# Hybrid backbone step on one core: loads and copies of the DeltaNet heads in another order, and the left half of the output projection begun inside the last head

## The reference, cut to what matters

```python
def deltanet_mixer(h, w_in, conv_w, a_log, dt_bias, norm_g, w_out, s0):
    proj = h @ w_in                                   # q, k, v, z of 8 heads, and gates
    qkv, z, ab = jnp.split(proj, [QKV_W, QKV_W + HV], axis=-1)
    qkv = jax.nn.silu(short_conv(qkv, conv_w))
    q, k, v = jnp.split(qkv, [HK, 2 * HK], axis=-1)
    ...
    o_f, s_f = chunk_gated_delta(q, k, v, g[:, :, 0], beta[:, :, 0], s0[:, 0])
    o_b, s_b = chunk_gated_delta(flip(q), flip(k), flip(v), flip(g[:, :, 1]), flip(beta[:, :, 1]), s0[:, 1])
    o = o_f + flip(o_b)
    o = o * lax.rsqrt(jnp.mean(o * o, axis=-1, keepdims=True) + EPS) * norm_g
    o = o * jax.nn.silu(z.reshape(B, L, N_HEADS, HEAD_V))
    y = o.astype(h.dtype).reshape(B, L, HV) @ w_out   # the output projection
    return y, jnp.stack([s_f, s_b], axis=1)

def run_trunk(x, cond, dn_state0, rows, p):           # layer 0 shown
    mod = jax.nn.silu(cond) @ p['ada_w'][i] + p['ada_b'][i]
    sh1, sc1, g1, sh2, sc2, g2 = jnp.split(mod[:, None, :], 6, axis=-1)
    y, s = deltanet_mixer(x * (1.0 + sc1) + sh1, ...)
    x = layer_norm(ALPHA * x + g1 * y, p['ln_g'][i, 0], p['ln_b'][i, 0])
    y = swiglu(x * (1.0 + sc2) + sh2, p['ffn_w_gu'][j], p['ffn_w_down'][j])
    x = layer_norm(ALPHA * x + g2 * y, p['ln_g'][i, 1], p['ln_b'][i, 1])
```

## Time and profile before

| | us |
|---|---|
| three runs | 2220.36, 2223.6, 2232.7 |
| median | 2223.6 |
| the profiled execution, whole | 2243.42 |
| its span (first to last instruction) | 2241.6 |
| PE busy | 1988.6 (89%) |
| DVE / ACT / POOL busy | 980.4 / 764.8 / 804.6 |
| mean granted clock of TensorE (1 is 2.4 GHz) | 0.955 |

### The profile page before, as it was taken

How to read it: one execution, slowest core, us unless ns; L and a number is a source line. 1 busy time by engine, 2 the same in 40 slices (tenths; PEclk the granted TensorE clock), 3 DMA queues, 4 the chain that set the end, 5 groups by cost and what they waited for, 6 DMA issues and landing times. The chain is left out here.

```text
span 2241.6 us, 39883 instructions
## 1 busy us (share of the span) xinstructions
PE 1988.6 (89%) x14992; PEld 1598.5 (71%) x14993; DVE 980.4 (44%) x1616; ACT 764.8 (34%) x1243; POOL 804.6 (36%) x486
## 2 busy tenths in 40 slices
PE   5889899899898699999999998889998898899990
PEld 2778778778787546888788876668786686677770
DVE  3345555555566345432322238443233333332228
ACT  2323323333333102222122202364445545544331
POOL 0054243342353203212111133564346546543234
PEclk7999999999999899999999999999999999999995
DMA  8132232332331424324322441785658758765354
GB/s 275 29 107 86 84 107 67 103 108 63 107 100 47 174 104 140 98 81 144 104 94 85 133 142 51 249 291 188 191 178 260 245 177 273 226 198 161 114 174 155
DMA packets 264225, 320.08 MB, mean 143 GB/s; under 512 B 25801, under 2 KB 206289, under 8 KB 263979
## 3 DMA queue, kind: packets, MB, share of 16 engines
q1 hardware_dynamic: 249115, 284.95, 39.9%
q10 hardware_dynamic: 10832, 16.96, 2.1%
q0 software_dynamic: 4032, 14.68, 1.7%
HBM read 283.87 MB, written 32.65 MB: 141 GB/s over the span
## 5 line engine op out<-in xcount | busy, mean ns | idle before, releaser
L1349 POOL TENSOR_TENSOR wlo<-wring,whi 128x1024 fp32r<-128x1024 f32 x182 | 460.2, 2531 | 768.5 <-ACT whi L1824 704.2
L1140 PE MATMUL pp<-whi,xTh 128*128 128x512 f32 (+1 forms) x1152 | 448.3, 389 | 40.1 <-POOL wlo L1349 13.1
L1824 ACT ACTIVATE whi<-wring 128x1024 fp32r<-128x1024 f32 (+1 forms) x324 | 316.0, 982 | 452.0 <-PE pp L1142 364.1
L1142 PE MATMUL pp<-wlo,xTh 128*128 128x512 f32 (+1 forms) x1152 | 432.9, 376 | 0.0
L1141 PE MATMUL pp<-whi,xTl 128*128 128x512 f32 (+1 forms) x1152 | 432.3, 375 | 0.0
L2431 DVE TENSOR_TENSOR wlo<-wring,whi 128x1024 fp32r<-128x1024 f32 (+1 forms) x180 | 222.5, 1236 | 214.3 <-ACT whi L1824 126.5
L1140 PEld LDWEIGHTS pp<-whi,xTh 128*128 128x128 f32 x1152 | 219.4, 190 | 96.3 <-issue 32.1
L1142 PEld LDWEIGHTS pp<-wlo,xTh 128*128 128x128 f32 x1152 | 219.0, 190 | 39.9
L1141 PEld LDWEIGHTS pp<-whi,xTl 128*128 128x128 f32 x1152 | 219.9, 191 | 34.5
L1140 PE MATMUL pp<-whi,hTh 128*128 128x512 f32 x528 | 212.7, 403 | 9.2 <-POOL wlo L1349 3.1
L1142 PE MATMUL pp<-wlo,hTh 128*128 128x512 f32 x528 | 206.6, 391 | 0.0
(11 more groups left out here) (327 smaller groups left out, 2964.6 us busy)
## 6 DMA issues: line engine op xcount, KB each, us to landing
wring<-in_moe_w_gu SPq DMA_DIRECT2D x320, 256.0 KB, 3.8
wring<-in_ada_w SPq DMA_DIRECT2D x80, 512.0 KB, 4.9
wring<-in_moe_w_down SPq DMA_DIRECT2D x160, 256.0 KB, 3.5
wring<-in_ffn_w_gu SPq DMA_DIRECT2D x80, 256.0 KB, 3.1
wring<-in_dn_w_in SPq DMA_DIRECT2D x128, 128.0 KB, 2.9
wring<-in_ffn_w_down SPq DMA_DIRECT2D x40, 256.0 KB, 3.1
expert_in<-zeros SPq DMA_DIRECT2D x36, 256.0 KB, 3.3
wring<-in_ada_w SPq DMA_DIRECT2D x32, 256.0 KB, 5.5
```

Source lines behind the costliest of these rows:

```text
L1140: pe.matmul(out, hi[:, c0 + c, tt], wh, start=(first and c == 0), stop=False)
L1142: mm = pe.matmul(out, hi[:, c0 + c, tt], wl, start=False, stop=(last and c == nk - 1))
L1349: pool.tensor_tensor(wlo[:, hs, 0:nk, 0:w], wring[:, ring_p.slot(k), 2:2 + nk, 0:w], whi[:, hs, 0:nk, 0:w].bitcast(F32), ALU.subtract).the ...
L1824: act.activation(whi[:, hs, 0:nk, 0:w], wring[:, ring_v.slot(k), 2 * s:2 * s + nk, 0:w], ACT.Copy)\
```

## The change

Four parts.

1. **SP**: the fills behind steps b = 0, 1, 2, 3 are now behind b = 0, 1, 3, 4; b = 2 has none. Where the list of chunks ends (in heads 6 and 7), three loads of `w_out` take the places.
2. **ACT**: `chunk_high` of the first chunk of head h + 2 moves from `scan(h)` into `inversion(h)`, behind the last `vt_copy` and ahead of `z_silu`; that of the second moves to the end of `scan(h)`, ahead of `out_square`.
3. **POOL and DVE**: `chunk_low` of the second chunk of each head moves from POOL to DVE, behind `update(h, 3)` of the inversion in which it is used.
4. **Output projection**: `w_out` is loaded by half slots (row pairs of two heads, 512 KB). A unit `out_unit(n, t, h)` is one matmul 128x512. For the left half, heads 0 to 5, tiles 0 to 3: 12 units stand where the projection of a next head would, in `inversion(7)`, and 12 between the steps of `scan(7)`. Tile 4 follows the scan, ahead of `out_columns(7)`; head 6 behind it, head 7 once `oT` is complete. The right half is unchanged in order, with banks of its own, so that only tile 3 waits for DVE (for all of the left residuals). The right weights of heads 4 to 7 are loaded once the units of tile 4 are done.

```diff
+def out_bank(n, t):
+    return (5, 7, 4, 6, 0)[t] if n == 0 else (1, 2, 3, 0, 4)[t]
...
@@ SP @@
             for hd in range(H):
-                for b in range(BURSTS):
+                for b, ahead in enumerate((2, 3, None, 4, 5)):
                     i = 2 * (BURSTS * hd + b) + RING
                     ada_loads(i, min(i + 2, 2 * BURSTS * H))
-                    q = CHUNKS * (hd + 1) + b + 2
-                    if b < CHUNKS and q < CHUNKS * H:
+                    q = CHUNKS * (hd + 1) + (ahead or 0)
+                    if ahead and q < CHUNKS * H:
                         chunk_fill(q)
+                    elif ahead and q < CHUNKS * H + RING:
+                        k = q - CHUNKS * H
+                        sp.wait_ge(S["slot_free"], 2 * (KD + CHUNKS * H + k + 1))
+                        out_load(k, 0, 0, 2 * k)
+            sp.wait_ge(S["ada_ps"], 1 + BURSTS * H)
+            out_load(0, 1, 0, 6)
+            out_load(1, 1, 1, 0)
+            out_load(2, 1, 1, 2)
...
@@ PE, inversion @@
                 def proj(lo, hi):
                     if nx:
                         project(h + 1, lo, hi)
+                    else:
+                        out_early(12 * lo // 32, 12 * hi // 32)
@@ PE, scan @@
                 adds(h, 0)
+                early(0, 2)
...
                 reads(h, 1)
+                early(2, 3)
...
@@ PE, after the heads @@
+            for h in range(6):
+                mm = out_unit(0, T - 1, h)
+            mm.then_inc(S["slot_free"], 4)
             out_columns(H - 1)
+            out_loaded(0, 1)
+            pe.wait_ge(S["oT_ready"], H)
+            for t in range(T):
+                out_unit(0, t, 6)
...
             pe.wait_ge(S["oT_ready"], H + 1)
-            for a in range(2):
-                gemm5(a, 4, lhs_o, 4 * a, a == 0, a == 1, S["res_ps"])
+            for t in range(T):
+                out_unit(0, t, H - 1).then_inc(S["res_ps"], 1)
...
             for t in range(T):
-                pe.wait_ge(S["res_step"], 2 * (t + 1))
+                if t == 3:
+                    pe.wait_ge(S["res_step"], 2 * T)
@@ POOL @@
                 if h + 2 < H:
                     chunk_low(CHUNKS * (h + 2))
-                    chunk_low(CHUNKS * (h + 2) + 1)
@@ ACT, inversion @@
                 vt_copy(h, 13)
+                if h + 2 < H:
+                    chunk_high(CHUNKS * (h + 2))
                 if nx:
                     z_silu(h + 1)
@@ ACT, scan @@
-                if h + 2 < H:
-                    chunk_high(CHUNKS * (h + 2))
-                    chunk_high(CHUNKS * (h + 2) + 1)
...
                     q_squares(h + 1)
+                if h + 2 < H:
+                    chunk_high(CHUNKS * (h + 2) + 1)
                 out_square(h)
@@ DVE, inversion @@
                 update(h, 3)
+                if nx:
+                    chunk_low(CHUNKS * (h + 1) + 1)
```

More of the change, by code:

```diff
@@ L540, in _ @@
             sp.dma_start(x[:, 1:T, :], A["x_sample"][0].rearrange("(t p) d -> p t d", p=P)).then_inc(S["x_in"], 16)
[L541 to L545, removed]
+            for half in range(2):
+                out_skip(3, half)
+            sp.wait_ge(S["slot_free"], 2 * RING + 2 * (KD + CHUNKS * H) + 4)
+            for k in (4, 5):
+                out_load(k, 0, 1, 2 * k - 4)
+                out_skip(k, 1)
+            ring.base += CHUNKS * H + OUT_SLOTS
             def zero_rows(e, k):
@@ L677, in slot @@
                 return ring.slot(k)
[L679 to L691, removed]
             pe.wait_ge(S["consts_in"], 16)
@@ L923, in out_columns, with out_loaded, out_unit, out_early @@
                 mm.then_inc(S["ogT_ps"], 1)
+            out_ring = Ring()
+            out_ring.base = KD + CHUNKS * H
+            def out_loaded(k, half):
+                pe.wait_ge(slot_loaded[out_ring.slot(k)][half], out_ring.loaded(k))
+            def out_unit(n, t, h):
+                k, row = out_weight(n, h)
+                return pe.matmul(bank(out_bank(n, t)), oT[:, h, t * P:(t + 1) * P], wring[:, out_ring.slot(k), row, :],
+                                 start=(h == 0), stop=(h == H - 1))
+            def out_early(lo, hi):
+                for i in range(lo, hi):
+                    t, h = i // 6, i % 6
+                    if i == 0:
+                        pe.wait_ge(S["ex_ready"], 4 * H)
+                        pe.wait_ge(S["v_ready"], H)
+                        pe.wait_ge(S["oT_ready"], 6 + 1)
+                    if i < 6 and h % 2 == 0:
+                        out_loaded(h // 2, 0)
+                    out_unit(0, t, h)
             def inversion(h):
@@ L999, in scan, with early @@
                 nx = h + 1 < H
+                def early(lo, hi):
+                    if not nx:
+                        out_early(12 + lo, 12 + hi)
                 pe.wait_ge(S["r_ready"], h * 4 + 4)
@@ L1016, in scan @@
                 adds(h, 1)
+                early(3, 5)
                 if nx:
@@ L1019, in scan @@
                 reads(h, 2)
+                early(5, 6)
                 if nx:
@@ L1022, in scan @@
                 adds(h, 2)
+                early(6, 8)
                 if nx:
@@ L1025, in scan @@
                 reads(h, 3)
+                early(8, 9)
                 if nx:
@@ L1028, in scan @@
                 adds(h, 3)
+                early(9, 11)
                 if nx:
@@ L1031, in scan @@
                 reads(h, 4)
+                early(11, 12)
                 if nx:
@@ L1078, in _ @@
             pe.wait_ge(S["oT_ready"], H + 1)
-            for a in range(2):
-                gemm5(a, 4, lhs_o, 4 * a, a == 0, a == 1, S["res_ps"])
+            for t in range(T):
+                out_unit(0, t, H - 1).then_inc(S["res_ps"], 1)
             pe.wait_ge(S["res_ps"], T)
-            pe.sem_inc(S["slot_free"], 2)
-            s2, s3 = slot(2), slot(3)
+            pe.sem_inc(S["slot_free"], 4)
             for t in range(T):
-                pe.wait_ge(S["res_step"], 2 * (t + 1))
-                for k in range(KD):
-                    mm = pe.matmul(bank(t), lhs_o(k, t), wring[:, s3 if k > 3 else s2, k % 4, :], start=(k == 0), stop=(k == KD - 1))
+                if t == 3:
+                    pe.wait_ge(S["res_step"], 2 * T)
+                for h in range(H):
+                    if t == 0 and h % 2 == 0:
+                        k, row = out_weight(1, h)
+                        out_loaded(k if h < 4 else k + RING, row // 2)
+                    mm = out_unit(1, t, h)
                 mm.then_inc(S["res_ps"], 1)
@@ L1425, in _ @@
             chunk_low(0)
-            chunk_low(1)
             pool.wait_ge(S["gate_step"], 12)
@@ L1430, in _ @@
             chunk_low(CHUNKS)
-            chunk_low(CHUNKS + 1)
             for h in range(H):
```

41 lines of the change are left out of this document (28 added, 13 removed).

## The result

The changed kernel takes 2173.77 us (median of 4 runs, 2172.05 to 2176.81) against 2228.15 for the kernel before on the same chip: ratio 0.9759, 95% interval 0.9721 to 0.9797, 54.4 us less. The forecast was 56.5 less and 2167, the range 2151 to 2189.

What follows compares the result with a forecast made beforehand. Heads 0 to 5 were held bound by burst and copy waits with slow matmuls behind, the end by DVE and its row loads. Heads -43, last head +4.5, end -18: -56.5 from 2223.6, forecast 2167 us, range 2151 to 2189.

Steps and rivals of the forecast that it cites:

- The burst wait: Heads 0 to 5: PE waits 20.7 us ahead of fifth bursts, their ada loads queued behind SP's third fill; would go.
- contention with the later fill: Fifth burst's load in each head: margin 1.6 us less some contention with a fill 3 us later; taken as zero.
- the rival of a busy memory: Heads 0 to 5: the 20.7 us are the load itself and stay; total -26.5, 2197 us; chance 0.08.
- The copy wait: Scans of heads 0 to 5: 13.9 us, as two `chunk_high` on ACT precede the copy `gram_k` needs; would go.
- The standstill of DVE: Heads: DVE blocked beside POOL, 0.8 us per head at three convolution products, 0.3 at the moved `chunk_low`.
- the strict reading: DVE and POOL port lock: moved subtractions and neighbours could cost DVE some 2 us more per head, 12 in sum.
- The last head: Head 7 with 24 units inside: inversion +2.7, scan +5.7, 4 taken back by the clock; 4.5 us more, bounds 0 and 11.
- The 4 us of clock: Head 7, inversion and scan: fewer PE pauses would win back 4 of some 6 us lost to slow matmuls.
- Behind the last head: From the scan's end to tile 4's residual: start falls from S + 79.9 to about S + 62, 18 us less.
- the bound set to none: Row loads behind the last head: 1 MB of right weights beside them could delay them up to 4 us; none taken.
- Part 4 as a whole: Output projection: last head 4.5 us more, 18 us less behind it; the end gives 13.5.
- The 20 us: Whole kernel: the profiled execution (2243.4) lay 20 us above the runs' median, 2223.6; the sum was set against the median.

Runs made afterwards that it cites:

- the SP order alone: Only SP's order of the fills changed, against the kernel before: 2192.91 against 2224.71, ratio 0.9862.
- second profile of before: The kernel before, unchanged, profiled once more: that execution took 2220.1 us, the median beside it 2224.71.
- heads alone: SP's fill order and the chunk copies and subtractions changed, old output projection kept, against the kernel before: 2179.49 us, ratio 0.9797.
- the projection alone: The kernel before with only the new output projection, fills and chunk copies as before: 2227.54 against 2228.71, ratio 0.9985.
- the kernel with the later products: The changed kernel with DVE's six row products moved behind the five left residuals: 2162.31 us, ratio to before 0.9718.
- the fastest kernel: The changed kernel with DVE's row products behind the left residuals and POOL's `chunk_low` ahead of `k_scale`: 2158.24 against 2222.03, ratio 0.9705.

## Why the prediction was right, point by point

- **The burst wait** went entirely, by the queue's order, as the SP order alone shows (32 us of the 45). No contention with the later fill was found: each fifth burst starts without a wait. Right, and the rival of a busy memory is out.
- **The copy wait** fell from 13.9 to 2.6 us over six heads (0.3 in each of heads 1 to 5, 0.9 in head 0). Neither moved `chunk_high` costs anything: ACT's stays of 1.06 us end at 553.55 and 585.59, and PE's waits name neither.
- **The standstill of DVE** was taken as 0.8 and 0.3 us per head; it is 0.54 at the three products (3.27 against 2.73) and nothing for PE at the other place. There `chunk_low` on DVE takes 1.22 us, but `out_gated` behind it takes 1.89 us where it takes 0.83 alone, and POOL's pair of products 4.08 where the next pair takes 2.49; nobody on PE waits for either. So DVE loses 1.6 us per head in all (1.1 taken, and 2 by the strict reading), but only 0.54 of it lies on PE's path. Heads: 43 forecast; 43.8 to 47.4 in the profiles, by which execution of before is taken, and 45 by the medians of the kernel without part 4.
- **The last head** was to cost 4.5. It costs 3.0 against the first profile of before and 7.0 against the second. The second is the one to go by, since all four other profiles with the old projection show 37.8 to 38.4 us of inversion and none the 42.4 of the first. So this term was too small by 2.5. Inversion: +3.7 (2.7 forecast). Scan: its step grew from 2.96 to 4.36 us as worked out, four times 1.4, but it is only 3.4 longer, since its first 40 matmuls, now at full clock, take 4.70 us instead of 6.84. The 4 us of clock came as busy time of PE, but only some 2 of them shorten the path; the prediction took off all 4. In the second profile of before (windows of the inversion and the scan) PE is busy for 25.39 + 16.90 us:

```profile
708.26:746.10 37.84, 25.39 (x726) 19.32 (x726) 21.12 (x41) 4.99 (x13) 20.66 (x19) 0.88 0.32 103
746.10:766.92 20.82, 16.90 (x112) 15.40 (x112) 8.27 (x32) 3.37 (x6) 0.00 (x0) 0.89 0.85 310
```

  After it is 35.50 + 23.28: 16.5 more for 24 units that are 20.6 at full clock, so 4.1 came back. The scan's first 40 matmuls in the two (timelines):

```profile
746.10 6.84 PE L752 MATMUL pp<-scratch 128*128 128x128 f32 x40 [0.66 <-DVE scratch L2171]
```

```profile
705.17 4.70 PE L775 MATMUL pp<-scratch 128*128 128x128 f32 x40 [0.66 <-DVE scratch L2249]
```

- **Behind the last head** 18 was too much: 15.0. The mechanism held, with PE's pause of 12.03 us (10.5 forecast) released by DVE. The step that failed is the bound set to none: the rows come 2.8 us later (23.1 us behind the scan's end, 20.3 before), because not only the right weights but everything behind them in SP's queue moves up. And 1.0 us more go to the slow matmuls after the pause (8.01 against 7.03), plus 0.9 for the first transposes (1.97 against 1.04 to 1.09); the sum had no slow matmuls there. From the rows to the end of `h_row(0)` DVE took 24.2 us instead of the 25.4 worked out, which took some of it back.
- **Part 4 as a whole** was priced at 13.5 as if it could be had by itself. By itself it gives 1 to 3 us; in the changed kernel it gives some 8, since heads alone are at 0.9797 and all four parts at 0.9759. The two intervals just touch, but head 7 and the stage behind it agree: 138.5 us in the profile with the old projection, 130.5 in the changed kernel. The prediction saw that the fills of head 7 were replaced by loads of `w_out`, but did not follow them through the old order of SP, where they would have blocked head 6's fifth burst.
- **The 20 us** by which the profiled execution of before lay above the median were for the most part in the rest: 1387.1 us behind residual(1, 4) against 1371.2 in the next profile, with 3.5 more in heads 0 to 5 and 4.0 in head 7. To set the sum against the median was right.
- **The total** came within 2 us of the forecast partly by luck. By the medians of the heads and the stages it is -45 + 7 - 15 = -53, against -43 + 4.5 - 18: the heads gave 2 more, the last head cost 2.5 more, the end gave 3 less. The bounds were also added up wrong: those named (0 to 3 us per head, 0 to 1, last head 0 to 11) reach from 2156 to 2191, not from 2152 to 2186, and leave out the 1 us per head that the text sets for the second `chunk_high` (2197 with it). The measured time lies inside either.
- **Open:** the rest. It takes 1377 to 1379 us in the changed kernel and the variants with its projection, 1372 and 1374 in the two fastest of them and 1383.5 in the projection alone; with the old projection it takes 1370 to 1374, but for the 1387.1 of the first profile. The first SwiGLU has 1 to 3 us of it where it was read. The ring of weights is entered at another slot there; whether that is the cause wasn't tried. For the same reason the stages don't add up to the medians exactly: against the second profile of before they give -43.8 + 7.0 - 15.3 = -52.1, the rest +6.7 and the start -0.8, in all -46.2, the difference of the two spans; that execution was 4.6 us under the median of its kernel. The 54.4 is a figure of medians, and the split among stages is known to some 5 us.

## What to carry to other kernels

A wait that the profile puts down to "issue" ahead of a matmul that reads loaded data can be a load queued behind another that waits for something else: set the issue time in the DMA queue beside the start of the reader, and when a queue's order is changed or new transfers are put in, follow each wait that now stands ahead of an urgent load, in every iteration, those at the end too. Before PE work is moved forward, look which engine bounds the place that it leaves: here DVE waited for all eight row loads to do work that needed only the first two, and moving one block of DVE gave 12 us, the whole early half of the projection some 8. Fillers put early between the steps of a recurrence lengthen it (3 to 4 us for 12 units here), and give nothing back while PE has a pause later on that could hold them: here the kernel's median was 7 us lower without them.

## What the runs showed of the hardware that was not expected

**A fall of the clock without a longer pause ahead of it.** Some heads take 79.83 instead of 78.30 us with the same waits. In the kernel with the later products, the 4 us on both sides of the border between heads 3 and 4, and of that between heads 4 and 5 (windows, columns as above):

```profile
427.68:431.68 4.00, 3.47 (x32) 3.27 (x30) 2.94 (x9) 3.08 (x5) 1.28 (x2) 1.00 0.00 0
431.68:435.68 4.00, 4.00 (x21) 3.16 (x21) 3.60 (x7) 0.31 (x1) 1.69 (x1) 0.66 0.52 142
...
507.51:511.51 4.00, 3.47 (x31) 3.27 (x30) 2.94 (x9) 3.09 (x5) 1.27 (x2) 1.00 0.00 0
511.51:515.51 4.00, 4.00 (x29) 3.16 (x29) 3.59 (x7) 0.31 (x1) 1.69 (x1) 1.00 0.57 147
```

PE was busy for 3.47 us of the four ahead of the border in both places. In the one the granted clock then is 0.66 (part of the stretch at 1.2 GHz), in the other it stays at 1.00. It costs 1.53 us. Heads 1 to 6 of both profiles of the changed kernel have none of it, the profile shown and four others have one, and that of the fastest kernel two, each time in the first 4 us of a head and with a clock of 0.66 to 0.70 there. What sets it off is not known. It comes and goes between executions of kernels whose heads are the same, so edits worth 2 to 3 us can't be read from a total.

**DVE and POOL hold each other up both ways.** Beside each other `out_gated` on DVE takes 1.89 instead of 0.83 us and POOL's pair 4.08 instead of 2.49:

```profile
521.19 1.89 DVE L2267 TENSOR_TENSOR scratch<-scratch,ss 128x640 f32<-128x640 f32 x1
...
520.12 4.08 POOL L1482 TENSOR_TENSOR scratch<-big,gates 128x640 f32<-128x640 f32 x2
525.84 2.49 POOL L1482 TENSOR_TENSOR scratch<-big,gates 128x640 f32<-128x640 f32 x2
```

POOL loses 1.6 us to `chunk_low` and `out_gated` (0.6 of it already in the kernel before, where the pair took 3.09 us), DVE 1.1. The prediction counted only what DVE loses; neither reached PE here.
